# The gate of the second block: half of one plus a hyperbolic tangent in place of addition, reciprocal and a GpSimd product

## The reference, cut to what matters

```python
def mixer_a(x, w_in, w_out, cos, sin):
    h = x @ w_in
    ...                                   # three dilated groups of banded attention, merged by softmax
    z = h[..., -A_WIDTH_2:]
    return (o * jax.nn.silu(z)) @ w_out

def mixer_b(x, w_in, sinks, w_out, cos, sin):
    q, k, v, z = split_cols_2(x @ w_in, [B_WIDTH, B_KV_2, B_KV_2, B_WIDTH])
    ...                                   # banded attention, 16 query heads on 2 key heads, sinks
    return (o * jax.nn.silu(z)) @ w_out

# in second_block, for each layer i:
    x = layer_norm(DEEPNORM_ALPHA * x + h, ln_g[i], ln_b[i])
    gate = jax.nn.sigmoid(x @ ple_w_gate[i])
    x = x + gate * (p[i] @ ple_w_proj[i])
```

## Time and profile before

| | |
|---|---|
| time, median of 3 runs | 1852.92 us (1852.1 to 1853.34) |
| the profiled execution's own time | 1848.8 us |
| its span (first to last instruction) | 1847.4 us |
| PE busy | 1667.7 us (90%) |
| DVE busy | 1083.8 us (59%) |
| ACT busy | 652.0 us (35%) |
| POOL busy | 527.6 us (29%) |
| mean granted TensorE clock | 0.961 |
| chain that ended last | PE 70%, DVE 20%, issue 5%, ACT 3% |

### The profile page before, as it was taken

The page is one execution under the profiler, slowest core; times in us unless marked ns, Lnnn a source line. Parts: engine busy times, 40 slices in busy tenths (PEclk is TensorE's granted clock), DMA queues, the critical chain, the costliest instruction groups (busy, mean ns, idle before and its releaser), DMA issues.

```text
span 1847.4 us, 24335 instructions
## 1 busy us (share of the span) xinstructions
PE 1667.7 (90%) x9336; PEld 1327.4 (72%) x9336; DVE 1083.8 (59%) x2019; ACT 652.0 (35%) x1247; POOL 527.6 (29%) x394
## 2 busy tenths in 40 slices
PE   7999998989888889989999899869999998987888
PEld 5555555467766668856657899869998888776676
DVE  4579888379999963333334788554444544226721
ACT  2433242142323232233333555434444443125401
POOL 1011110127676620013220011015665654013301
PEclk9999999999999989999999899989999999998989
DMA  9234332334444442302222455443443333342231
GB/s 342 102 114 148 107 117 89 111 113 160 166 153 171 152 155 92 103 29 78 72 69 80 151 184 183 159 153 111 150 135 126 127 125 103 103 161 95 69 103 57
DMA packets 63954, 231.69 MB, mean 125 GB/s; under 512 B 7408, under 2 KB 8432, under 8 KB 63584
## 3 DMA queue, kind: packets, MB, share of 16 engines
q1 hardware_dynamic: 61376, 220.75, 35.0%
q0 software_dynamic: 1744, 4.72, 0.8%
q10 hardware_dynamic: 720, 4.68, 0.6%
HBM read 229.08 MB, written 1.05 MB: 125 GB/s over the span
## 4 chain that ended last, share of the span: by engine, by line
PE 70%; DVE 20%; issue 5%; ACT 3%; POOL 0%; DMA 0%; DVEq 0%; ACTq 0%; POOLq 0%
PE ps L218 17%; PE ps L236 6%; DVE junk L307 6%; PE ps L238 6%; PE ps L237 6%; DVE ring L310 4%; PE ps L1185 3%; PE ps L1187 3%; PE ps L1186 3%; PE ps L1600 3%; PE ps L710 3%; PE ps L226 3%; PE ps L700 3%; PE ps L603 2%; PE ps L365 2%
## 5 line engine op out<-in xcount | busy, mean ns | idle before, releaser
L236 PE MATMUL ps<-h_hi,weights_rounded 128*128 128x512 f32 (+1 forms) x656 | 224.9, 343 | 36.3 <-POOL weights_rest L257 34.1
L245 ACT ACTIVATE weights_rounded<-ring 128x1024 fp32r<-128x1024 f32 x196 | 204.5, 1051 | 107.3 <-PE ps L1187 107.1
L251 DVE TENSOR_TENSOR weights_rest<-ring,weights_rounded 128x1024 fp32r<-128x1024 f32 x130 | 167.8, 1295 | 120.4 <-ACT weights_rounded L245 120.4
L257 POOL TENSOR_TENSOR weights_rest<-ring,weights_rounded 128x1024 fp32r<-128x1024 f32 x66 | 196.2, 2985 | 137.7 <-ACT weights_rounded L245 137.7
L237 PE MATMUL ps<-h_lo,weights_rounded 128*128 128x512 f32 (+1 forms) x656 | 223.3, 340 | 0.0
L238 PE MATMUL ps<-h_hi,weights_rest 128*128 128x512 f32 (+1 forms) x656 | 223.2, 340 | 0.0
L218 PE MATMUL ps<-h,ring 128*128 128x512 f32 (+1 forms) x496 | 196.9, 554 | 7.1 <-DVE h L456 7.1
L218 PEld LDWEIGHTS ps<-h,ring 128*128 128x128 f32 x496 | 95.5, 195 | 100.6 <-issue 92.4
L236 PEld LDWEIGHTS ps<-h_hi,weights_rounded 128*128 128x128 f32 x656 | 126.4, 193 | 57.0 <-issue 38.7
L310 DVE SCALAR_TENSOR_TENSOR ring<-ring,cond_rows 128x1024 f32<-128x1024 f32 x80 | 162.0, 2026 | 2.8
L218 PE MATMUL ps<-mix,ring 128*128 128x256 f32 (+1 forms) x512 | 144.1, 445 | 13.0 <-DVE mix L953 4.7
(11 more groups left out here) (247 smaller groups left out, 3411.8 us busy)
## 6 DMA issues: line engine op xcount, KB each, us to landing
ring<-in_up SPq DMA_DIRECT2D x88, 512.0 KB, 3.6
ring<-in_ada_rest SPq DMA_DIRECT2D x80, 512.0 KB, 3.7
ring<-in_a_in SPq DMA_DIRECT2D x80, 512.0 KB, 3.5
ring<-in_down SPq DMA_DIRECT2D x44, 512.0 KB, 3.5
ring<-in_even SPq DMA_DIRECT2D x20, 512.0 KB, 3.5
ring<-in_ada_first SPq DMA_DIRECT2D x16, 512.0 KB, 8.0
ring<-in_wout SPq DMA_DIRECT2D x16, 512.0 KB, 3.5
ring<-in_odd SPq DMA_DIRECT2D x16, 512.0 KB, 3.5
```

The lines of the kernel that those rows point to most:

```text
L236: te.matmul(bank[:, 0:n], wh[:, k, :], hi(k), start=k == 0, stop=False)
L245: sc.activation(pair[0], place(*key), ACT.Copy).then_inc(*mark("rounded", *key))
L251: ve.tensor_tensor(pair[1], place(*key), pair[0].bitcast(F32), ALU.subtract).then_inc(*mark("rest", *key))
L257: po.tensor_tensor(pair[1], place(*key), pair[0].bitcast(F32), ALU.subtract).then_inc(*mark("rest_pool", *key))
```

## The change

The gate uses sigmoid(z) = (1 + tanh(z/2)) / 2. ACT writes tanh(z/2) into `sg` and z/2 into `z`; DVE makes (sg + 1) * z in one `scalar_tensor_tensor`, for which it now waits on both of ACT's results. `pool_gate` is gone. Because the mixers' tables become the set "exp_and_others", which holds no logarithm, `act_close` loads "natural_log_exp_and_others" at its start (two more table loads in the program).

```diff
-        sc.activation(sg, bank[:, 0:SEQ], ACT.Exp, scale=-1.0).then_inc(*mark("z_exp", *key))
-        sc.activation(z, bank[:, 0:SEQ], ACT.Copy).then_inc(*mark("z_copied", *key))
-
-    def dve_gate(key, sg):
-        ve.wait_ge(*at("z_exp", *key))
-        ve.tensor_scalar(sg, sg, 1.0, None, ALU.add).then_inc(*mark("sigmoid_sum", *key))
-        ve.wait_ge(*at("sigmoid_sum", *key))
-        ve.reciprocal(sg, sg).then_inc(*mark("sigmoid", *key))
-
-    def pool_gate(key, sg, z):
-        po.wait_ge(*at("z_copied", *key))
-        po.wait_ge(*at("sigmoid", *key))
-        po.tensor_tensor(z, z, sg, ALU.mult).then_inc(*mark("z_gated", *key))
+        sc.activation(sg, bank[:, 0:SEQ], ACT.Tanh, scale=0.5).then_inc(*mark("z_tanh", *key))
+        sc.activation(z, bank[:, 0:SEQ], ACT.Copy, scale=0.5).then_inc(*mark("z_copied", *key))
+
+    def dve_gate(key, sg, z):
+
+        ve.wait_ge(*at("z_tanh", *key))
+        ve.wait_ge(*at("z_copied", *key))
+        ve.scalar_tensor_tensor(z, sg, 1.0, z, ALU.add, ALU.mult).then_inc(*mark("z_gated", *key))
...
-            sc.preload_act_table_set("natural_log_exp_and_others")
+            sc.preload_act_table_set("exp_and_others")
...
     def act_close(layer):
+        sc.preload_act_table_set("natural_log_exp_and_others")
         sc.wait_ge(*at("ln_mean", layer))
...
     def act_mixer_b_pre():
-        sc.preload_act_table_set("natural_log_exp_and_others")
+        sc.preload_act_table_set("exp_and_others")
...
-            dve_gate(("b", i, f), SGB[f])
+            dve_gate(("b", i, f), SGB[f], ZB[f])
...
-        pool_gate(("b", i, 0), SGB[0], ZB[0])
-        pool_gate(("b", i, 1), SGB[1], ZB[1])
```

More of the change, by code:

```diff
@@ L1538, in dve_mixer_a @@
         weigh_copies(ve, 0, A, packs(us), TBA, PTA)
-        dve_gate(A, sga)
+        dve_gate(A, sga, za)
         ve.wait_ge(*at("z_gated", *A))
@@ L1560, in pool_mixer_a @@
         rest(i + 1, 2)
-        pool_gate(("a", i), sga, za)
     mu, rs = SCR[:, 0:256], SCR[:, 256:512]
```

## The result

The changed kernel took 1839.1 us (median of 6, 1835.74 to 1843.46), the kernel before in the same series 1852.51 (6, 1851.79 to 1853.34): a ratio of 0.9929, 95% interval 0.991 to 0.9947, 13.2 us by the ratio. No run took 1839.1 us: three took 1835.74 to 1836.0 us and three 1842.19 to 1843.46, and the median is the middle between the two groups. I had forecast 1844.7 us, 8.2 us less, between 1842.0 and 1849.0. Two later series of the same changed kernel, further down, gave medians of 1842.2 and 1842.3 us and 0.995 (0.9937 to 0.9963) and 0.995 (0.9936 to 0.9964), that is 9.3 us. The three intervals overlap. So the question is not only where the time went but which of these numbers is the change.

A forecast was written before the change was run, and what follows sets the result against it. PE, busy 90%, was taken as the bound, so gains come only where it waits at the mixers' ends: 2.23 + 3.36 + 1.7 + 0.9 = 8.2 us off the 1852.92 median gives 1844.7 us, range 1842.0 to 1849.0.

The forecast's parts named there:

- Only three gates of sixteen are on the path: Both mixers: PE waits only for the gates where a mixer ends, one in mixer_a and two in mixer_b.
- Price of tanh and of the fused pass: ACT's tanh takes 0.38 us like the exponential; DVE's fused pass takes 0.42 us, between 0.28 and 0.48.
- A, 2.23 us: End of mixer_a: the last product into MIX starts 2.23 us sooner, 2.17 to 2.37.
- B, 3.36 us: End of mixer_b: the last product into MIX starts 3.36 us sooner, then held by PE's weighing.
- my lower case: End of mixer_b: gain of 2.9 us if the weighing's later half ended half a microsecond later than its row says.
- The added table loads and the earlier subtractions, at nothing: Two loads of 1283 ns fall in ACT's waits; DVE's earlier subtractions stay within slack; cost nothing.
- The collision: DVE's earlier subtraction beside POOL's L257 may cost POOL 1.1 us, within a slack of 2.5 to 2.9 us.
- The clock at A, 1.7 us: Start of the first close: with PE's wait cut to 1.7 us the granted clock no longer falls, winning 1.7 us.
- rival (3): Gain partly given back: each further low clock stretch costs 1.7 us; one leaves 1849.0, two 1850.7; chance 0.15.
- The clock at B, 0.9 us: Second close: the clock rises sooner after PE's shorter wait, worth 0 to 1.9 us; the middle, 0.9, taken.
- rival (1): As forecast, with 0 to 1.9 us from the clock at mixer_b's end: 7.3 to 9.2 us won; chance 0.55.
- the same difference: Whole kernel: the profiled execution stays 4.1 us from the median, so the gain came off the median of 1852.92 us.

The follow-up runs named there:

- each mixer alone: The new gate in one mixer only, against the kernel before: in mixer_a alone 1846.04 us, ratio 0.9973; in mixer_b alone 1846.39 us, ratio 0.997.
- the delay: Changed kernel with two more DVE instructions ahead of mixer_a's last product into MIX, putting PE's wait back: 1846.27 us, ratio to the kernel before 0.9977.
- the filling: Kernel before, old gates, with 28 PE products of no use in the wait at the end of mixer_a: 1848.46 us, ratio 0.9984.

## Why the forecast missed, step by step

**Only three gates of sixteen are on the path: right.** PE's waits inside mixer_a are unchanged to the tenth, its units are as long as before, and each mixer alone gave about half.

**Price of tanh and of the fused pass: right**, 384 and 420 ns for 380 and 420.

**A, 2.23 us: right**, 2.18.

**B, 3.36 us: right in the mechanism, the size depends on the clock.** 2.94 us (6.29 - 3.35) in two executions, where the last product into MIX started 0.47 us behind the weighing's last row and not the 0.04 that I had put, which is my lower case; and 3.81 in one where the clock had risen in the weighing, which I had not counted. By the same 0.4 us PE's wait there is 0.9 to 1.0 us and not 0.5. The whole stage of mixer_b gave 3.7 on average: it took 117.5 us in the profile that I worked from and 119.2 in two others of the old gate, so by the first alone it gave 2.6 and by the others 4.3.

**The added table loads and the earlier subtractions, at nothing: right.** The collision did come, and hit DVE: its subtraction beside POOL's took 2.59 us in place of 1.22, with POOL's unchanged at 2.41.

```profile
1323.04 2.41 POOL L257 TENSOR_TENSOR weights_rest<-ring,weights_rounded 128x1024 fp32r<-128x1024 f32 x1 [2.29 <-ACT weights_rounded L245]
```

```profile
1323.94 2.59 DVE L251 TENSOR_TENSOR weights_rest<-ring,weights_rounded 128x1024 fp32r<-128x1024 f32 x1 [0.93 <-ACT weights_rounded L245]
```

I had stretched the wrong engine, POOL, which began first and kept its length. PE used the result later than either and waited for neither.

**The clock at A, 1.7 us: right**, shown from both sides by the delay and by the filling. Of six profiles with the long wait at A five have output products of 29.58 us and one, with the new gate in mixer_b alone, 30.89: there the fall cost 3.0. And what a later stretch like that at 1610 us costs, 1.7 us in rival (3), was too much: with it the first close took 75.23 us, without it 74.31, which is 0.9. **The clock at B, 0.9 us: about right on average**, 1.9 to 2.7 in one execution of three and 0.2 to 1.0 in two.

**Sum: 8.2 us; measured by the second block's length 9.3, by the two later series 9.3.** Undersized are B, by 0.4, the clock at B, by 0.6, and the clock at A, by 0.3; A is over by 0.2. My rival (1), 1843.7 to 1845.6, is missed by 1.4 us by the later medians, 1842.2 and 1842.3. They lie inside the whole range, at its low end.

**What failed is the last step, from the sum to the median and its range**, and in it the premise that "the same difference" lies between profile and median, with all that stands ahead of 1231 us fixed. Its first sign was in the times shown: the profiled execution of before was 4.1 us below a median whose three runs lay within 1.3 us. I took that for an offset of the profile. There is no such offset: in later series the profiled execution was 0.5 and 1.7 us below the median of its series and once 2.5 above it. It was the spread of single executions: 1846.0 to 1854.7 us over the 67 runs of the kernel before beside the later series, and 1230.6 to 1237.4 us for an unchanged first block. Low stretches of the clock that come or not are a part of it, in the first block too: of these 67 runs and the 12 of the kernel before again, those with a mean granted clock of 0.957 took 1852.5 to 1854.4 us and those with 0.962 or more 1846.0 to 1852.1. They are not shown to be all of it, since runs at 0.960 alone took 1849.1 to 1854.7.

In the changed kernel's first profile the stretch of the trace on which I rested the claim that waits up to 1.9 us leave the clock alone has such falls itself (0.98 over 201 us is two of 3.4 us, at 549 and at 600 us):

```profile
450.00:651.00 201.00, 175.57 (x743) 140.16 (x741) 198.70 (x191) 63.58 (x80) 137.11 (x48) 0.98 0.47 166
549.00:553.00 4.00, 4.00 (x12) 3.15 (x11) 3.96 (x4) 0.00 (x0) 1.68 (x1) 0.57 0.08 12
```

The stretch was at 1.00 in the earlier trace rows, and below it in seven of the fourteen profiles. So that row was one draw. For A it gave the right answer in every profile taken; as a rule it was too strong, and my rival (3) put stretches that come or go at 0.15 where in the profiles they are a main part of the spread.

The 13.2 us of the first series are then the 8.2 of the sum, 1.1 that the stages gave beyond it, and 3.9 that no later series showed. Single executions are spread by 4 us to each side. With that added to the range of 1842.0 to 1849.0 its low end is 1838, and 1839.1 lies in it. But that is the width for one execution: the five medians of the kernel before lie between 1850.4 and 1852.5. So a wider range was called for, and a median as low as 1839.1 still came by two groups of which I had no row.

What stays open: why the first series had a group at 1836 us that eleven later runs, on two chips, had not.

## What to carry to other kernels

Gates, norms and other small chains cost what they keep the busiest engine waiting only where a stage ends; look there, and count sixteen instances as three if thirteen are covered. Price such a wait together with the clock it costs behind it, here 1.7 us behind 3.9 of waiting, and ask whether keeping PE busy with work of no use would win part of it: at the two places alone the filling won 3.0 and 2.0 us with the old gate, and in all the longer waits of the second block 12 us on top of the edit's 9. And before a forecast of less than 1% compare the profiled execution with the timed median: a gap between them is a sign of spread, which the range must hold. Look at the single times too: a median between two groups is a time that no execution took.

## What was not expected of the hardware

Products of no use pay: 32 of them in each unit of mixer_b brought the clock over that mixer from 0.85 to 0.98 and took 5.6 us off; with the longer waits of the second block filled the kernel is 1.2% faster than before.

Of two engines whose two-operand passes overlap in time, the one that began first kept its length and the other was stretched, in the places looked at: DVE's subtraction took 2.59 us for 1.22 when POOL had begun its own 0.9 us earlier, and ended 1.08 us after it; POOL's sum took 1.76 us for 0.74 (1333.28 in the profile before) when DVE had begun a subtraction 0.06 us earlier, and ended 0.59 us after it. Where both began at 1336.52, POOL's was stretched to 1.82. The stretched pass ends a little less than its own length behind the other, as if it had stood meanwhile. No run isolated it.
